# Where fp32r tiles begin in SBUF: every one at the same place of 512 bytes, on one Trainium2 core

## What is computed

```python
# first block
proj = h @ w_in + b_in                      # 1024 -> 4616 columns: xm, om, gates, us, ga, gb
q, k = einsum(xc, w_mlstm_q), einsum(xc, w_mlstm_k)     # chunked mLSTM
y_a = (hm * gain * sigmoid(om)) @ w_mlstm_down          # operand g
val, gate = split(ys @ w_s5_glu)                        # operand ys
y = sigmoid(ga) * y_a + sigmoid(gb) * y_b
mix = y @ w_mix_out                                     # operand y
val, gate = split(h @ w_ffn_up)
f = (gelu(conv(gate)) * val) @ w_ffn_down               # operand act
# second block
y = rmsnorm(h) @ w_in;  h += concat([att, conv]) @ w_out
xq = rmsnorm(h) @ w_xq                                  # operand x
xk, xv = rmsnorm(mem) @ w_xk, rmsnorm(mem) @ w_xv       # operand mn
h += xo @ w_xo                                          # operand xo
u = rmsnorm(h) @ w_up
h += square(relu(u)) @ w_down                           # operand u
```

## The kernel before

| tiles | before | after |
|---|---|---|
| `x_tok`, `h_hi`, `h_lo`, `raw`, `w_hi`, `w_lo` | 128 | 128 |
| `ys`, `y`, `g_hi`, `act`, `x`, `xo`, `u` (hi and lo), `tail_m`, `tail_f`, `tail_u` | 192 | 128 |
| `g_lo`, `mn_hi`, `mn_lo` | 448 | 128 |
| float32 tiles at `X` plus a multiple of 128 (`xmT`, `xcT`, `usys`, `rows_m`, `rows_f`, `att_area`, `rel`, `xqT`) | 192 | 128 |
| `mv` / `sm` / `grow` | 0 / 128 / 192 | 320 / 0 / 64 |

## Time and profile before

### The profile page before, as it was taken

The page is one execution under the profiler, slowest core; times in us unless marked ns, Lnnn a source line. Parts: engine busy times, 40 slices in busy tenths (PEclk is TensorE's granted clock), DMA queues, the critical chain, the costliest instruction groups (busy, mean ns, idle before and its releaser), DMA issues.

```text
span 1638.8 us, 19089 instructions
## 1 busy us (share of the span) xinstructions
PE 1586.3 (97%) x7532; PEld 1293.7 (79%) x7532; DVE 750.5 (46%) x1344; ACT 636.6 (39%) x1139; POOL 673.1 (41%) x518
## 2 busy tenths in 40 slices
PE   4999999999998999999999999999999999999998
PEld 4888857778887888888887788778878888888886
DVE  7879223546666443133207799852442421012103
ACT  3443554443425433133332434682442442224312
POOL 0663323234444544444455464003414444444442
PEclk9999999999999999999999999999999999999999
DMA  9393432249634344333333442002212332333322
GB/s 322 105 151 110 118 95 64 65 134 306 216 103 142 103 147 142 97 90 104 91 115 95 130 116 82 22 1 78 88 41 77 103 103 93 101 90 91 102 94 73
DMA packets 221673, 180.29 MB, mean 110 GB/s; under 512 B 24200, under 2 KB 184328, under 8 KB 221456
## 3 DMA queue, kind: packets, MB, share of 16 engines
q1 hardware_dynamic: 212368, 166.48, 34.9%
q10 hardware_dynamic: 9216, 12.60, 2.5%
HBM read 172.49 MB, written 6.55 MB: 109 GB/s over the span
## 4 chain that ended last, share of the span: by engine, by line
PE 88%; DVE 6%; ACT 2%; DMA 1%; POOL 1%; issue 1%; SPq 0%; DVEq 0%; ACTq 0%
PE bank L618 15%; PE bank L620 15%; PE bank L619 15%; PE bank L677 9%; PE bank L675 9%; PE bank L676 9%; PE bank L713 3%; PE bank L1050 1%; PE bank L1021 1%; PE bank L914 1%; DMA xmT<-in_w_ada 1%; POOL w_lo L2380 1%; PE bank L697 1%; PE bank L1107 1%; PE bank L698 1%; PE bank L699 1%
## 5 line engine op out<-in xcount | busy, mean ns | idle before, releaser
L2380 POOL TENSOR_TENSOR w_lo<-raw,w_hi 128x512 fp32r<-128x512 f32 (+1 forms) x492 | 649.4, 1343 | 919.6 <-ACT w_hi L1175 918.6
L1175 ACT ACTIVATE w_hi<-raw 128x512 fp32r<-128x512 f32 (+1 forms) x492 | 281.0, 621 | 343.1 <-PE bank L677 268.9
L618 PE MATMUL bank<-h_hi,w_hi 128*128 128x512 f32 x936 | 368.6, 394 | 2.2 <-POOL w_lo L2380 2.2
L620 PE MATMUL bank<-h_hi,w_lo 128*128 128x512 f32 x936 | 365.5, 391 | 0.0
L619 PE MATMUL bank<-h_lo,w_hi 128*128 128x512 f32 x936 | 365.5, 391 | 0.0
L618 PEld LDWEIGHTS bank<-h_hi,w_hi 128*128 128x128 f32 x936 | 176.4, 188 | 41.6 <-ACT usys L1237 2.6
L619 PEld LDWEIGHTS bank<-h_lo,w_hi 128*128 128x128 f32 x936 | 176.6, 189 | 37.2 <-issue 0.7
L620 PEld LDWEIGHTS bank<-h_hi,w_lo 128*128 128x128 f32 x936 | 176.5, 189 | 37.1
L2207 DVE SCALAR_TENSOR_TENSOR bank<-att_area,cols,bank 128x512 f32<-128x512 f32 x116 | 87.6, 755 | 3.9
L675 PE MATMUL bank<-w_hi,u_hi 128*128 128x512 f32 x224 | 88.6, 396 | 0.0
L676 PE MATMUL bank<-w_lo,u_hi 128*128 128x512 f32 x224 | 88.6, 396 | 0.0
(11 more groups left out here) (429 smaller groups left out, 2639.4 us busy)
## 6 DMA issues: line engine op xcount, KB each, us to landing
raw<-in_w_in SPq DMA_DIRECT2D x57, 512.0 KB, 4.1
raw<-in_w_ffn_up SPq DMA_DIRECT2D x44, 512.0 KB, 3.9
raw<-in_w_up SPq DMA_DIRECT2D x32, 512.0 KB, 4.0
raw<-in_w_down SPq DMA_DIRECT2D x32, 512.0 KB, 3.8
ada_ring<-in_w_ada SPq DMA_DIRECT2D x24, 512.0 KB, 5.8
raw<-in_w_ffn_down SPq DMA_DIRECT2D x20, 512.0 KB, 3.7
raw<-in_w_s_glu SPq DMA_DIRECT2D x16, 256.0 KB, 3.1
raw<-in_w_mlstm_down SPq DMA_DIRECT2D x8, 512.0 KB, 6.1
```

Source lines behind the costliest of these rows:

```text
L618: te.matmul(ps, wv[0][:, i, :], rh, start=(i == 0), stop=False)
L620: last = te.matmul(ps, wv[1][:, i, :], rh, start=False, stop=(i == kt - 1))
L1175: sc.activation(W_HI[SLOT[key]][:, part_], raw[:, RAW_SLOT[key], part_], ACT.Copy).then_inc(*hi_set.up((key, n_)))
L2380: gp_.tensor_tensor(W_LO[s_][:, part_], raw[:, RAW_SLOT[key], part_], W_HI[s_][:, part_].bitcast(F32), ALU.subtract).then_inc(*lo_made.up( ...
```

## The change

The start of the upper region, `X`, goes down by 16 elements (64 bytes), and the three tiles whose distance from `X` is no multiple of 128 elements go down by 64 more, so that all tiles of type fp32r begin 128 bytes past a multiple of 512. The room for it comes from `mv`, 32 elements, which moves from below `X` to the end of the memory. `sm`, `aeT` and `grow` close up. No instruction, no order, no wait and no transfer is added, removed or moved: on each of the five engines' lists of instructions nothing differs.

```diff
-            assert dt == F32 or (BASE + 4 * at) % 64 == 0, name
+            assert dt == F32 or at % P == 0, name
...
-        mv = place("mv", 24032, [16, 2])
-        sm = place("sm", 24064, [8, 16])
-        aeT = place("aeT", 24192, [TT, 36])
-        grow = place("grow", 24336, [D])[:, :]
-        X = 25360
+        sm = place("sm", 24032, [8, 16])
+        aeT = place("aeT", 24160, [TT, 36])
+        grow = place("grow", 24304, [D])[:, :]
+        X = 25344
+        mv = place("mv", X + 27824, [16, 2])
...
-        g_lo = place("g_lo", X + 23744, [KD, S], F32R)
+        g_lo = place("g_lo", X + 23680, [KD, S], F32R)
...
-        xkT = place("xkT", X + 25792, [KD, NMEM])
-        mn_hi = place("mn_hi", X + 23744, [KD, NMEM], F32R)
-        mn_lo = place("mn_lo", X + 21696, [KD, NMEM], F32R)
+        xkT = place("xkT", X + 25728, [KD, NMEM])
+        mn_hi = place("mn_hi", X + 23680, [KD, NMEM], F32R)
+        mn_lo = place("mn_lo", X + 21632, [KD, NMEM], F32R)
...
-        aa = place("att_area", X + 2048, [23704])
+        aa = place("att_area", X + 2048, [23680])
```

## The result

Over ten runs of each, the changed kernel takes 1629.85 us (1628.41 to 1633.26), the kernel before 1641.85 us (1632.79 to 1647.3). The ratio is 0.9929, 95% interval 0.991 to 0.9947: 0.7% faster, which is 11.7 us of the time before (8.7 to 14.8 by the interval; the medians differ by 12.0). Forecast were 11.7 us, 1628.9 us.

A forecast was written before the change was run, and what follows sets the result against it. PE's stream of matmuls was taken as the bound. Token stages 8.9, tails 0.8 and 0.1, feature stages 1.9 sum to 11.7 us: 1640.6 - 11.7 = 1628.9 us, range 1622 to 1638.

The forecast's parts named there:

- The bound: Whole kernel: PE, busy for 1586.3 of 1638.8 us, sets the time by its stream of matmuls.
- The size of a mismatch: Token products: a matmul on tiles at different places takes 233.3 ns, on equal places 226.8, so 6.5 ns each.
- token stages: Products on u, act, y and xo: 1368 matmuls gain 6.5 ns each, 8.9 us.
- The tails: Tails of mix, ud1 and fd1: 120 matmuls on weights give 0.8 us, 96 on tail tiles 0.1 us at best.
- The feature stages: Weights stationary: g gives 0.5 us, h between g blocks 0.3, x 0.5, ys 0.5; 1.9 us with the rounding.
- On mn: Key and value matmuls on mn: nothing counted, as they lie beside chains of other engines.
- My upper bound: 12.9 us in total, adding 1.2 us for the matmuls on mn should their cover be gone.
- float32, DVE, ACT, POOL: Plain float32 matmuls and the operations of DVE, ACT and POOL: indifferent to the tiles' places, gain nothing.
- (B): Rival: matmul rates depend on memory region, both tiles low or both high, not the remainder; time stays 1640.6 us; chance 0.12.
- (C): Rival: a tile's place has no effect, stationary and moving reads being independent; time stays 1640.6 us; chance 0.03.
- (D): Rival: moved float32 tiles make DVE's and ACT's accesses meet PE's; at 15% more an operation, 1649 us; chance 0.05.
- The mechanism as I put it: On PE, stationary loads and moving reads obstruct each other, least where both begin at the same place of 512 bytes.

The follow-up runs named there:

- w_apart: Changed kernel with only the weights' tiles w_hi and w_lo, and the small tables behind them, moved 64 bytes up; ratio to before 1.0121, median 1662.92 us.
- one_side: Changed kernel with u_lo moved 64 bytes up and act_hi 64 bytes down; u 231.0 ns a matmul, act 228.9 ns; no total time given.
- split: Changed kernel with u_hi 64, u_lo 256, xo_lo 64 and x_lo 192 bytes up; x distances 1.3 to 2.4 ns longer than 227.0; no total time given.
- experiments 2 and 3: Experiment 2 is w_apart; experiment 3 is the changed kernel with all of memory moved up by 32 bytes, ratio to before 0.9933.

## Why the prediction was right, and where it was only lucky or open

- **The total.** That 11.7 us came out to the decimal is luck: the interval goes from 8.7 to 14.8 us, the medians differ by 12.0 and the two profiled spans by 9.5, and the 1640.6 from which I started was the median of three runs, where ten give 1641.85. What isn't luck are the prices, which the traces show stage by stage: 9.0 + 0.8 + 0.3 + 1.6 = 11.7 us.
- **The bound.** PE's stream set the time, and what was taken from it came out at the end: 9.5 us of span, 10.6 from 367 us on, with 1.3 us lost to a transfer that scatters.
- **The size of a mismatch.** 6.5 ns in a token product was forecast; 233.3 to 226.7 ns was measured, 6.6. With the counts, the token stages gave 9.0 us (u 4.5, act 2.7, xo 1.2, y 0.6) against 8.9.
- **The tails.** 0.8 us on w were right; the tail tiles gave 0.3 us, not 0.1, as those of fd1 had been at 230.3 ns and the first twelve of ud1 at 230.6, and not at the 228.3 that I read in mix and took for all.
- **The feature stages.** Forecast 1.9 us, measured 1.6: x went from 229.2 to 227.1 ns over all its blocks, g from 229.5 to 226.9, ys from 229.3 to 227.6, and the blocks on h between those on g from 5.49 to 5.44 us. The 229.6 that I had for x was 18.6 us of rounded starts over only 81 matmuls. That h was held up by its neighbours, and that this would end, came out.
- **On mn.** Nothing was counted, since DVE's chain covers it; PE's wait there is 6.2 us, not longer than the 6.9 of the earlier trace rows as I had it. The 256-column matmuls became slower, not faster, 283 instead of 279 ns a record. The wait after, and the rows of L619 on mn before and after:

```profile
PE bank L713 <- ACT branch L1191: 6.2, 1, 6.2
```

```profile
L619 PE MATMUL bank<-mn_lo,w_hi 128*128 128x256 f32 x64 | 17.9, 279 | 0.0
```

```profile
L619 PE MATMUL bank<-mn_lo,w_hi 128*128 128x256 f32 x64 | 18.1, 283 | 0.0
```

  My upper bound counted on 3.3 ns of gain there; it would have been a loss of 2 ns a matmul between starts (118.2 to 120.3). It showed in no later wait, being covered.
- **float32, DVE, ACT, POOL.** Zero, as said. The groups of DVE that answer to the earlier trace rows, on h_hi, whose place stayed, and on x_hi, whose place moved:

```profile
L1671 DVE SCALAR_TENSOR_TENSOR h_lo<-bank,cols,h_hi 128x512 fp32r<-128x512 f32 x16 | 10.9, 744 | 20.5 <-ACT h_hi L1218 20.5
...
L1671 DVE SCALAR_TENSOR_TENSOR x_lo<-bank,cols,x_hi 128x512 fp32r<-128x512 f32 x8 | 5.5, 745 | 14.6 <-ACT x_hi L1218 14.6
```

- **The rivals.** (B), the region, falls with the changed kernel itself (u far above the weights, and 226.8 ns) and once more with `w_apart` (h and w in one region, 233.3). (C) falls with it. (D), writers in step with readers, would show in the rows above and in the busy times of DVE and ACT (750.5 and 750.4 us, 636.6 and 634.9), and doesn't.
- **The mechanism as I put it**, loads of the stationary tile against the moving tile's reads, is still only an argument: `w_apart` shows that the pair counts, `one_side` and `split` that neither simple form of it explains the single matmul. The forecast didn't hang on it, because it took its prices from stages that ran at either rate in the same trace. The words "of 512 bytes" were the change's, and I kept them without a test: the period is 256.

The page "TensorE: Matmul & The Clock Gate" of the Trainium skill, sections "Step-by-step: what each phase is for" and "Back-to-back issue gap", has two independent read ports, for the moving and for the stationary operand, and at 512 columns 216 ns for an isolated matmul and 131 ns in a stream of load and matmul pairs, with no term for the place. The runs don't agree for fp32r: 226.7 to 234.2 ns at 512 columns, by nothing but the tiles' addresses. Whether the two ports meet somewhere they don't show, as which reads collide is open.

## What to carry to other kernels

When two stages of one shape run at different rates beside the same neighbours, compare start-to-start distances and then the addresses of their tiles; a price found so, inside one trace, gave each group of stages to within 0.3 us, and the whole as near as the runs can tell. Let all fp32r tiles that meet in a matmul of 512 columns begin at one remainder of 256 bytes, slices included, and above all those of a long stream; which remainder is free (128 and 160 were tried with all tiles, 192 in the tails of before), so it can be had by shifting a region rather than by padding each tile. A near miss costs as much as a far one, and shifting the one tile that all products share can cost more than the whole gain (31 us between experiments 2 and 3, by their ratios).

## What the runs showed of the hardware that I had not expected

- A matched stream at 512 columns of fp32r takes 226.7 ns a matmul, an unmatched one 229 to 234.2, by the distance modulo 256 bytes and its sign; plain float32 matmuls take the same 0.43 us at the two distances that were seen, 0 and -64.
- A stream can run at two rates with the same tiles: 233.3 and 228.8 ns in the two halves of one stage of `w_apart`, one trace. Both halves come directly behind products at 233.3 ns; what decides is open. And twelve matched matmuls among mismatched ones ran at 230.8 ns there.
- At 256 columns, the mismatched tiles of mn (64 bytes apart over the period) ran faster than the matched ones, 118.2 against 120.3 ns between starts; in `w_apart`, apart by -64, they took 118.2 again.
- At -64, moving the stationary tile of one matmul in three costs two thirds of the whole (231.0 ns), moving those of two in three costs all of it (233.3).
